# Output gates of late tokens: projected inside three heads' scans, or after the first gather

## The reference, cut to what matters

```python
z = h @ p['w_in']
q, f_fw, f_bw, v, g, xr, xg, ga, gb = jnp.split(z, IN_SPLITS, axis=-1)
...
o = _rmsnorm(o, p['hg_norm']) * jax.nn.silu(heads(g))            # branch A, 4 heads of 128
y_a = o.reshape(b, n, HG_VW) @ p['w_branch_a']
...
hr = h_fw + _flip(h_bw)                                           # branch B, 512 channels
y_b = (hr.astype(h.dtype) * jax.nn.gelu(xg)) @ p['w_branch_b']
merged = jax.nn.sigmoid(ga) * y_a + jax.nn.sigmoid(gb) * y_b
return (merged @ p['w_out'], ...)
```

## Time and profile before

| | |
|---|---|
| median of 3 runs (lowest to highest) | 3926.62 us (3925.56 to 3928.87) |
| profiled execution, its own time | 3930.68 us |
| its span, first to last instruction | 3928.9 us |
| mean granted clock of TensorE | 0.873 |
| TensorE, VectorE busy | 74%, 71% |
| gathers, share of the 16 DMA engines | 74.8% |

### The profile page before, as it was taken

The page is one execution under the profiler, slowest core; times in us unless marked ns, Lnnn a source line. Parts: engine busy times, 40 slices in busy tenths (PEclk is TensorE's granted clock), DMA queues, the critical chain, the costliest instruction groups (busy, mean ns, idle before and its releaser), DMA issues.

```text
span 3928.9 us, 46427 instructions
## 1 busy us (share of the span) xinstructions
PE 2919.7 (74%) x16938; PEld 1323.1 (34%) x16938; DVE 2786.8 (71%) x6838; ACT 679.4 (17%) x1397; POOL 1322.8 (34%) x1174
## 2 busy tenths in 40 slices
PE   7999999988899997856666566556656666665555
PEld 4666665555444442222322222212212222221111
DVE  5644646766787786747888768877877886877555
ACT  3543542011122220000111111110111111101000
POOL 0000000023334443434444444444444444444443
PEclk9999999999899998978888878877878877887777
DMA  4001004579999999999999999999999999999998
GB/s 191 26 28 31 25 19 178 182 274 413 415 411 405 416 403 416 412 422 416 400 407 411 407 408 416 419 408 420 408 415 414 419 411 408 418 418 401 420 421 344
DMA packets 214040, 1343.26 MB, mean 342 GB/s; under 512 B 24722, under 2 KB 45714, under 8 KB 62898
## 3 DMA queue, kind: packets, MB, share of 16 engines
q0 software_dynamic: 165888, 1208.03, 74.8%
q1 hardware_dynamic: 46628, 129.65, 8.9%
q10 hardware_dynamic: 1296, 2.62, 0.2%
HBM read 1326.55 MB, written 13.67 MB: 341 GB/s over the span
## 4 chain that ended last, share of the span: by engine, by line
DMA 39%; PE 34%; DVE 12%; issue 10%; POOL 2%; ACT 1%; SPq 0%; POOLq 0%; DVEq 0%; ACTq 0%
DMA arena<-in_uv,mask_b 14%; DMA arena<-in_uv,ones 12%; PE ps L798 12%; DMA arena<-in_uv,mask_f 12%; PE ps L1484 10%; DVE arena L1317 4%; PE ps L663 3%; POOL arena L632 2%; PE ps L776 2%; DVE arena L1197 2%; PE ps L1478 2%; PE ps L694 1%; DVE arena L1157 1%; PE ps L1536 1%; DMA arena<-in_w_mod 1%
## 5 line engine op out<-in xcount | busy, mean ns | idle before, releaser
L798 PE MATMUL ps<-arena 64*64 64x512 f32 x9216 | 1446.5, 754 | 944.3 <-DVE arena L1197 924.4
L1317 DVE CUSTOM_DVE_ANT_0 arena<-arena 128x1024 f32<-128x1024 f32 x1152 | 1411.3, 1225 | 736.2 <-DMA arena<-in_uv,mask_b 285.1
L798 PEld LDWEIGHTS ps<-arena 64*64 64x64 f32 x9216 | 348.6, 156 | 1883.0 <-DVE arena L1197 1380.0
L632 POOL DMA_INDIRECT arena<-in_uv,ones x384 | 441.0, 1148 | 620.2 <-PE ps L798 485.3
L632 POOL DMA_INDIRECT arena<-in_uv,mask_f x384 | 445.4, 1160 | 582.4 <-PE ps L798 497.6
L632 POOL DMA_INDIRECT arena<-in_uv,mask_b x384 | 430.8, 1122 | 586.8 <-PE ps L798 502.2
L992 ACT ACTIVATE arena<-arena 128x2 f32<-128x2 f32 x576 | 117.1, 203 | 2642.0 <-DVE arena L1317 2641.8
L1484 PE MATMUL ps<-arena 128*128 128x384 f32 x1152 | 382.8, 488 | 1.8 <-DVE arena L1778 1.8
L1197 DVE TENSOR_SCALAR arena<-arena 128x64 f32<-128x64 f32 x1152 | 307.9, 310 | 0.4 <-ACT arena L992 0.3
L776 PE MATMUL ps<-arena 128*128 128x384 f32 x768 | 269.4, 498 | 0.0
L614 POOL IOTA arena<- 128x16 f32 x1 | 0.1, 145 | 789.3 <-PE ps L676 789.3
(11 more groups left out here) (216 smaller groups left out, 2360.5 us busy)
## 6 DMA issues: line engine op xcount, KB each, us to landing
arena<-in_w_mg SPq DMA_DIRECT2D x16, 1536.0 KB, 21.1
arena<-in_w_in SPq DMA_DIRECT2D x28, 512.0 KB, 3.4
arena<-in_w_mod SPq DMA_DIRECT2D x8, 1792.0 KB
arena<-in_w_mod SPq DMA_DIRECT2D x4, 2048.0 KB, 23.1
arena<-in_w_out SPq DMA_DIRECT2D x2, 4096.0 KB, 16.9
arena<-in_w_q SPq DMA_DIRECT2D x8, 1024.0 KB, 15.4
arena<-in_w_q SPq DMA_DIRECT2D x4, 2048.0 KB, 36.5
arena<-in_uv,ones POOLq DMA_INDIRECT x384, 10.6
```

Source lines behind the costliest of these rows:

```text
L632: nc.gpsimd.indirect_dma_start(out=RG[n % RING], out_offset=None, in_=uv, in_offset=bass.IndirectOffsetOnAxis(ap=EIDX[t % 3][:, s:s + 1], ...
L798: mm = nc.tensor.matmul(PS[c * HALF:(c + 1) * HALF, 2 * r + n, :], DG[rows, s, :], RG[s][rows, D + n * 512:D + (n + 1) * 512], start=(g == ...
L1317: ins = v.tensor_tensor_reduce(u, u, h2, 1.0, 0.0, ALU.mult, ALU.add, PRE[:, s % RING:s % RING + 1])
```

## The change

For heads 0, 1 and 2 the scan projects only the first chunk of g and xg, the rows of the early tiles (16 matmuls instead of 48; head 3 is as before). `part_of` says how many matmuls stand in each step: 1 in steps 6 to 9, 0 in 10 and 11, 2 in 12 to 17. The results of the branches are stored without the gate for the other 768 rows. Behind the first gather, `put_off` projects the 12 missing pieces (3 heads x 2 gates x 2 chunks, 96 matmuls of 128x384) in groups 21 to 42, ScalarE takes Silu or Gelu, and VectorE multiplies it onto the stored result. The weights, six blocks of 512 KB, are loaded again for it. The late merge and what follows begin eight groups later. Blocks are numbered by a table (`Z_NUMBER`) in place of a formula. Some loads of SyncE change places.

```diff
-MERGE_AT, MERGE_STEP = 35, 5
-MIX_AT, MIX_STEP = 117, 3
+PUT_AT, PUT_STEP, PUT_STEP_LATE = (21, 31), 4, 5
+MERGE_AT, MERGE_STEP = 43, 5
+MIX_AT, MIX_STEP = 125, 3
...
-LATE_AT = {3: 2 * GROUPS + 24}
+LATE_AT = {3: 2 * GROUPS + 32, 4: 3 * GROUPS + 12}
...
+def scan_units(h):
+
+    if h < PUT_OFF:
+        return [(h, B_G, 0), (h, B_XG, 0)]
+    return [(h, b, n) for b in (B_G, B_XG) for n in range(NCH)]
+
+
+def part_of(h, it):
+
+    quota = lambda n: 4 if h == PUT_OFF else 2 if n >= LRU_STEP + 1 else int(n < GATE_STEPS + 4)
+    first = sum(quota(n) for n in range(GATE_STEPS, it))
+    return first, first + quota(it)
...
+    def put_group(n):
+        first, then = PUT_AT
+        early = PUT_STEP * (then - first)
+        return first + n // PUT_STEP if n < early else then + (n - early) // PUT_STEP_LATE
...
+        def put_off(d, queries):
+            sp.wait_ge(q_r, queries)
+            for kind, b in enumerate((B_G, B_XG)):
+                sp.dma_start(PUT_IN[d][:, kind * 4:kind * 4 + 4],
+                             w_in[d, W_BLOCKS.index(b)].rearrange("p (r k) c -> p r (k c)", k=2)).then_inc(l_put[d], 16)
+
         sp.wait_ge(q_r, 7)
         piece(7)
+        put_off(0, 7)
+        put_off(1, 10)
         score_in(1, 0)
+        put_off(2, len(QUERY_ORDER))
...
+        def put_off(n):
+
+            u, k = divmod(n, KD)
+            d, kind, part = put_unit(u)
+            bank = (5, 7)[u % 2]
+            if k == 0:
+                pe.wait_ge(l_put[d], l_put0 + 32)
+                if u >= 2:
+                    pe.wait_ge(put_e, put_e0 + u - 1)
+                elif u == 1:
+                    pe.wait_ge(h2t_e, EARLY)
+            mm = nc.tensor.matmul(PS[:, bank, 0:CH], PUT_W(d, kind, k), hT[:, k, part * CH:(part + 1) * CH],
+                                  start=(k == 0), stop=(k == KD - 1))
+            if k == KD - 1:
+                mm.then_inc(put_r, 1)
...
+        for n in range(PUT_UNITS * KD):
+            b.at(put_group(n), lambda n=n: put_off(n))
...
+            A(PUT_TMP, PS[:, (5, 7)[u % 2], 0:CH], (ACT.Silu, ACT.Gelu_apprx_tanh)[kind]).then_inc(put_e, 1)
...
+            to = (oA, hB)[kind][:, d, part * CH:(part + 1) * CH]
+            v.tensor_tensor(to, to, PUT_TMP, ALU.mult).then_inc(put_m, 1)
...
-                    c, part = divmod(it - GATE_STEPS, 2)
-                    project(*late_chunk(c), range(part * KD // 2, (part + 1) * KD // 2))
+                    for n in range(*part_of(h, it)):
+                        project(*scan_units(h)[n // KD], (n % KD,))
...
-            v.tensor_tensor(hl, hl, I[0][:, N_CTX:T].rearrange("p (c r) -> p r c", r=GRID_H),
-                            ALU.mult).then_inc(lru_done, 1)
+            il = I[0][:, N_CTX:T].rearrange("p (c r) -> p r c", r=GRID_H)
+            gated = (TA - N_CTX) // GRID_W if h < PUT_OFF else GRID_H
+            ins = v.tensor_tensor(hl[:, 0:gated], hl[:, 0:gated], il[:, 0:gated], ALU.mult)
+            if h < PUT_OFF:
+                ins = v.tensor_copy(hl[:, gated:], il[:, gated:])
+            ins.then_inc(lru_done, 1)
```

More of the change, by code:

```diff
@@ L68 @@
 NB = len(W_BLOCKS)
-ZC = B_END * NCH
+PUT_OFF = HEADS - 1
 TI = 2 * TILES
@@ L108, with z_numbers, z_done @@
 QUERY_AT = lambda n: 1 + 3 * (n - 2)
-MERGE_AT, MERGE_STEP = 35, 5
-MIX_AT, MIX_STEP = 117, 3
+PUT_AT, PUT_STEP, PUT_STEP_LATE = (21, 31), 4, 5
+MERGE_AT, MERGE_STEP = 43, 5
+MIX_AT, MIX_STEP = 125, 3
 EARLY_TOP_AT = {(0, 0): None, (0, 1): 0, (0, 2): 18, (0, 3): 27, (1, 0): 37, (1, 1): 47, (1, 2): 65, (1, 3): 78,
                 (2, 0): 90, (2, 1): 100, (2, 2): 110, (2, 3): 129}
-LATE_AT = {3: 2 * GROUPS + 24}
+LATE_AT = {3: 2 * GROUPS + 32, 4: 3 * GROUPS + 12}
 LATE_GAP = {3: 10}
-def late_chunk(c):
-    return (B_G, B_XG)[c // NCH], c % NCH
+def scan_units(h):
[6 more added lines that the diff above has]
+    return first, first + quota(it)
+assert all(part_of(h, TI - 1)[1] == len(scan_units(h)) * KD for h in range(HEADS))
+def z_numbers():
+    order = []
+    for h in range(HEADS):
+        order += [(h, b, n) for b in range(B_FF, B_G) for n in range(NCH)]
+        order += scan_units(h)
+    return {u: c for c, u in enumerate(order)}
+Z_NUMBER = z_numbers()
+Z_ALL = len(Z_NUMBER)
+def z_done(h, b):
+    return 1 + max(c for (hh, bb, n), c in Z_NUMBER.items() if (hh, bb) == (h, b))
 def wait_alone(eng, sem, value):
@@ L307, in build @@
     PIECE_IN = (2, 3, 0, 1, 4, 2, 3, 0)
+    PUT_IN = [MG[:, :, TA + n * PIECE:TA + (n + 1) * PIECE] for n in (1, 2, 0)]
+    PUT_W = lambda d, kind, k: PUT_IN[d][:, kind * 4 + k // 2, (k % 2) * P:(k % 2 + 1) * P]
+    PUT_TMP = AR[:, A_SIG:A_SIG + CH]
     KEYS_IN = strips[:, 8:16, 0:PIECE]
@@ L971, in stage_b_act @@
             b.at(at + 5, lambda n=n: scores_out(n))
+        for u in range(PUT_UNITS):
+            b.at(put_group(u * KD + KD - 1) + 1, lambda u=u: put_off(u))
         for c in range(2 * KD):
@@ L1041, in stage_b_dve, with put_off @@
             v.tensor_tensor(MROW2[u], PS[0:2, 4 * u + 3, :], BROW2[u], ALU.add).then_inc(m_evac, 1)
+        def put_off(u):
+            d, kind, part = put_unit(u)
+            dve.wait_ge(put_e, put_e0 + u + 1)
+            to = (oA, hB)[kind][:, d, part * CH:(part + 1) * CH]
+            v.tensor_tensor(to, to, PUT_TMP, ALU.mult).then_inc(put_m, 1)
         def merge_late(c):
@@ L1282, in stage_b_dve @@
                     b.at(top_at(t, i) + n, step)
+        for u in range(PUT_UNITS):
+            b.at(put_group(u * KD + KD - 1) + 2, lambda u=u: put_off(u))
         for c in range(2 * KD):
@@ L1459, in z_bank, with bank_of, project @@
             def z_bank(b, n):
-                c = h * ZC + b * NCH + n
+                return bank_of(h, b, n)
+            def bank_of(hz, b, n):
+                c = Z_NUMBER[hz, b, n]
                 if c >= 2:
                     pe.wait_ge(z_free, c - 1)
-                return z_of(h, b, n)
-            def project(b, n, ks=range(KD)):
+                return z_of(hz, b, n)
+            def project(hz, b, n, ks=range(KD)):
                 if ks[0] == 0:
-                    pe.wait_ge(l_w[W_BLOCKS.index(b)], h * 16 + 16)
-                    z_bank(b, n)
-                z = z_of(h, b, n)
+                    pe.wait_ge(l_w[W_BLOCKS.index(b)], hz * 16 + 16)
+                    bank_of(hz, b, n)
+                z = z_of(hz, b, n)
                 w = W[:, W_BLOCKS.index(b)]
@@ L1481, in project @@
                     for k in ks:
-                        if h == 0 and b == B_FF:
+                        if hz == 0 and b == B_FF:
                             pe.wait_ge(h_ready, n * KD + k + 1)
@@ L1671, in fill_out @@
                         ins.then_inc(z_free, 1)
-                elif (it - GATE_STEPS) % 2:
-                    b, n = late_chunk((it - GATE_STEPS) // 2)
+                    return
+                lo, hi = part_of(h, it)
+                for c in range(lo // KD, hi // KD):
+                    _, b, n = scan_units(h)[c]
                     out, func = ((oA, ACT.Silu), (hB, ACT.Gelu_apprx_tanh))[b == B_XG]
@@ L1939, in _ @@
                 oc = oA[:, h, n * CH:(n + 1) * CH]
-                v.scalar_tensor_tensor(out=oc, in0=turned(n), scalar=pr[:, h, P_HN:P_HN + 1], in1=oc,
-                                       op0=ALU.mult, op1=ALU.mult).then_inc(hg_done, 1)
+                if n and h < PUT_OFF:
+                    ins = v.tensor_scalar(oc, turned(n), pr[:, h, P_HN:P_HN + 1], None, ALU.mult)
+                else:
+                    ins = v.scalar_tensor_tensor(out=oc, in0=turned(n), scalar=pr[:, h, P_HN:P_HN + 1], in1=oc,
+                                                 op0=ALU.mult, op1=ALU.mult)
+                ins.then_inc(hg_done, 1)
         stage_b_dve(dve)
```

56 lines of the change are left out of this document (36 added, 20 removed).

## The result

| | before | changed |
|---|---|---|
| median (lowest to highest), 5 runs each, one chip | 3926.62 us (3925.56 to 3933.55) | 3948.72 us (3942.21 to 3954.20) |
| profile: span, mean granted clock | 3928.9 us, 0.873 | 3952.5 us, 0.876 |

The ratio is 1.0049, with a 95% interval of 1.0034 to 1.0064. The changed kernel is 22 us slower. I had said 3929 us and a range of 3915 to 3942, with no change as the likeliest case: this is wrong, on the slow side.

A forecast was written before the change was run, and what follows sets the result against it. It took TensorE work to bound the part up to the first gather and the DMA engines the rest. 3930.7 - 17.1 + 8.7 + 11.3 = 3933.6, on the median's level 3929.5; stated as 3929 us, range 3915 to 3942.

The forecast's parts named there:

- What bounds the kernel: Whole kernel: TensorE work bounds the part up to the first gather; afterwards only bytes moved and idle DMA time count.
- The scans, -17.1: Scans of heads 0 to 2: fewer filler matmuls gain 5.7 us a head, 17.1 us for three heads.
- its first item: Scan, shares of step 6 to shares of step 11: 20.38 us become 15.75, a gain of 4.6 us a head.
- rival 3: Scans: ScalarE's table load and exp hold lighter steps near 4 us; +16.7 us, 3943 us, chance 0.05.
- The pauses to come are below the first, so I expect no fall.: Clock: coming TensorE pauses are shorter than an earlier one of 1.93 us, so no fall is expected.
- Rival 4: Scans: the clock falls to 1.2 GHz in the light steps; +47 us, 3974 us, chance 0.03.
- The loads, +8.7: Gather part: six added loads of 512 KB, 3.15 MB at 0.363 MB per us, cost 8.7 us.
- Idle DMA, +11.3: Groups 21 to 30: TensorE's lateness leaves the DMA engines idle, 19.7 - 3.0 - 2.9 - 2.5 = 11.3 us.
- The excess of 19.7 us: Groups 21 to 30: TensorE needs 71.3 us where the groups took 51.6, 19.7 us more than the DMA engines need.
- The two deductions for loads (2.9 and 2.5): Idle DMA in groups 21 to 30: second pair of new loads fills 2.9 us; third pair and first merge weights 2.5.
- the deduction of 3.0 for the stock of issued gathers: Idle DMA in groups 21 to 30: gathers land 10.0 us after issue in the median, 7.0 at least; 3.0 us of stock.
- Rival 2: Groups 21 to 42: TensorE's lateness comes through whole, 19.7 us, plus 3 us later; +14.3 us, 3941 us, chance 0.14.

The follow-up runs named there:

- The scans alone: Changed kernel without the late chunks' projection, multiplication and loads for heads 0 to 2, later schedule as before; leaves out needed work: 3918.09 us, ratio 0.9966.
- both kernels from group 31 on: Changed kernel with put-off work in groups 31 to 50, merge from 51: 3975.08 us; the same with two pairs of SyncE's loads changed over: 3931.80 us.
- three groups later: Changed kernel with put-off work in groups 24 to 33, four matmuls a group, merge from 46, SyncE's loads reordered: 3935.79 us, ratio 1.0013.
- shorter rows: Changed kernel with its six put-off weight blocks loaded in rows of 512 B instead of 1 KB, same bytes: 3953.17 us, ratio 1.0054.
- the put-off work alone: Changed kernel with all 48 fillers kept in each scan, put-off matmuls, loads and later schedule unchanged: 3964.86 us, ratio 1.0085.
- the version that beats both: Against the kernel before: heads 0 to 2 put off two of six gate chunks, 48 matmuls in groups 31 to 40, three loads: 3919.35 and 3915.49 us.
- the one with the fourth head: Three-load version putting off two chunks per head, with head 3 also: 64 matmuls in groups 31 to 43, four loads, merge from 44: 3920.76 us, 0.9973.
- The zero matmuls: Changed kernel with products by a zero matrix added in scan steps 6 to 11, two fillers in each: 3948.98 us, ratio 1.0045.
- The kernel from group 31 on: Changed kernel with put-off work in groups 31 to 50, merge from 51, needed score loads ahead of waiting merge weights: 3931.80 us, ratio 1.0001.

## Why the prediction was wrong

**What bounds the kernel: right.** Two parts, TensorE and VectorE up to the first gather, the DMA engines behind it. The scans alone brought what they won in the first part to the end, and idle DMA came back at the end as time.

**The scans, -17.1: mis-sized, measured -11.4 and -15.4.** The working was right in its first item: from the shares of step 6 to those of step 11 it took 15.42 us (434.02 to 449.44 in the third head) where I had 15.75. So rival 3, ScalarE holding the light steps, is out, although the heads are more than 144 us apart, which I had named as its sign. The failed step is that on the clock: "The pauses to come are below the first, so I expect no fall." I held single pauses against the 1.93 us of the earlier trace rows, but these came in step after step. Not every such row brought a fall. The pauses of 0.62 us in steps 0 to 5 and those of 0.40 to 0.79 us in the steps with one filler left the clock at 1.00 in both traces. Each fall in these scans stands behind one of 1.43 to 1.77 us, and some pauses of 1.44 to 1.77 us had none behind them. So the length of a pause alone does not say whether the clock falls, and what does is open.

Rival 4 named this mechanism and priced it at 27 us of loss in three heads and none of the gain, 44 us worse than the forecast. It was 5.7 and 1.7 us worse in the two traces, because the clock was low for 3 to 10 us at a time and not for six steps, and because the fall is paid in full only where TensorE sets the pace. Against 142.46 us a head without any fall, a head with falls in its scan alone took 143.25; one behind the last outputs cost another 1.6 to 1.7 us (12.07 and 12.21 for 10.52). That two executions of the same kernel differ by 4 us here goes with where the second fall comes, which no experiment set.

What shows the cause: the clock fell in the scans of every kernel with the light steps, in all seven traces of them (the changed kernel twice, the scans alone, both kernels from group 31 on, three groups later, shorter rows). It never fell in scans in which TensorE waited at most 0.62 us from step to step (before, the put-off work alone), nor in those with at most 0.63 us and once 1.18 before the last outputs (the version that beats both, twice, and the one with the fourth head). The scans of the version that beats both took 17.6 us less than before, where 17.1 had been worked out for the lighter ones. The zero matmuls took the fall out of the steps that they filled and not out of the later ones, where TensorE still waited up to 1.60 us. The rule that the prediction quoted from the Trainium skill, "TensorE: Matmul & The Clock Gate", section "A second HAM failure mode: psum-queue depth-cycling", was the better guide here, and the trace agrees with it: short idles between groups of matmuls, 0.50 granted behind them.

**The loads, +8.7: right, slightly low.** The queue that carries them held this share of the DMA engines between 934 and 981 us of the changed kernel:

```profile
q1 hardware_dynamic: 2096, 2.10, 13.8%
```

2.10 MB for 6.5 us of all engines, 0.324 MB a us where the earlier trace rows had 0.363, so 3.15 MB cost 9.7.

**What was missing: when the loads land.** The prediction priced the bytes of the new loads and not the time until the first of them is there. This is the second failed step. Nothing in it said when TensorE would want them: issued behind 1 MB of query weights at 933.6, in a queue beside gathers that fill the engines, and wanted at 970.7. I read the landing times of the gathers, 10 us, and asked for none of a load on SyncE's queue. The wait took 10.41 us of TensorE's time (13.2 in the second trace) just where it was about to be the slower one, and beginning three groups later gave 13.2 back, which is not the wait's alone.

**Idle DMA, +11.3: 18.8.** The excess of 19.7 us was a good figure: I had given TensorE 71.3 us for groups 21 to 30, and groups 22 to 30 took 66.0, so 7.3 a group where 7.1 was worked out. The two deductions for loads (2.9 and 2.5) came in: 19.7 - 5.4 = 14.3, and 14.2 us were idle, with 5.6 us of loads beside them. What failed is the deduction of 3.0 for the stock of issued gathers, and 4.6 us were idle at the wait itself. That the wait had used the stock up fits this, but no run shows it by itself. Rival 2 had nearly this outcome (19.7 of idle time) with another reason, and it would have been slower by 14 us and not by 18 to 22.

**The sum.** -9.6 us up to the first products of a gather (856.35 and 846.73 us in the two timelines; 1.7 of the 11.4 are lost again from the merge on), +9.7 for the loads and +18.8 idle are +18.9. The spans of the two traces differ by 23.6 us, so 4.7 remain. In the second trace of the changed kernel it is -13.3 + 9.7 + 19.8 = +16.2 (first products at 843.10; 4.3 and 15.5 us idle) of 22.4, so 6.2 remain. By the medians the change cost 22.1 and 18.3 us. The kernel from group 31 on, with 14.4 against 9.7 for the loads alone, leaves 4.7 too. What this is stays open: groups 31 to 42 took 5.68 us each in the changed kernel where I had 5.30 and added nothing, but no run took them apart. The larger part of my error is behind the first gather, where I had +20.0 us and the traces have +33.2 and +35.6; the clock in the scans is the smaller part.

## What to carry to other kernels

When work is taken off an engine that then runs behind another, ask what its regular pauses do to its clock, and take only as much as the other engine's loop has room for: here half of the change, placed later, won 12 to 15 us, where all of it lost 18 to 22 as it was and nothing when placed later. A moved piece of work whose operands are loaded again needs two prices, the bytes and the time to landing in a full DMA system, and where such work begins matters as much as how much of it there is: a hole in the DMA engines' work seems to cost little where loads that are due anyway fall into it, which was read from the queue here and not isolated. Moving work later also moves the loads behind it in an in-order queue: look at what else stands in that queue before you call it free.

## What the hardware did that I had not expected

- The granted clock of TensorE fell to 0.50 in all three heads, behind pauses of 1.43 to 1.77 us that followed others in steps of about 3 us. A single pause of 1.93 us had no such effect. In two executions of one kernel the falls came in other places, and the scans took 518.8 and 515.0 us.
- A load of 1 MB on SyncE's queue, behind another of 1 MB, needed 47 us from its first issue to its landing beside gathers that filled the DMA engines: 45 GB/s for both loads, of some 410. Rows of 512 B for the second made it 52 us and not 69.
